# Gate matmuls of a recurrent mixer: one FP32 pass against three F32R passes over split operands

## What is computed

```python
xr = dwconv(xr, lru_conv_w[l], lru_conv_b[l], LRU_CONV_LEFT)      # 4 taps, per channel
xb = xc.reshape(b_, t_, LRU_BLOCKS, LRU_BLOCK_W)
r = jax.nn.sigmoid((jnp.einsum('btnk,nkj->btnj', xb, wa).reshape(b_, t_, ch) + ba).astype(jnp.float32))
i = jax.nn.sigmoid((jnp.einsum('btnk,nkj->btnj', xb, wx).reshape(b_, t_, ch) + bx).astype(jnp.float32))
log_a = -LRU_C * r * jax.nn.softplus(-lam.astype(jnp.float32))
a = jnp.exp(log_a)
b = jnp.sqrt(-jnp.expm1(2.0 * log_a)) * i * xc.astype(jnp.float32)
# then a scan  h = a * h + b  over context and latent tokens, in either direction
```

## Time and profile before

| | |
|---|---|
| median of the runs | 2164.99 us |
| profiled execution | 2164.49 us, span 2162.7 us |
| PE busy | 2083.7 us (96%) |
| DVE busy | 1572.5 us (73%) |
| ACT busy | 1059.2 us (49%) |
| POOL busy | 345.8 us (16%) |
| share of the last chain: PE, DVE, ACT | 79%, 11%, 4% |
| mean granted clock of TensorE | 0.995 of full speed |
| L890, 192 matmul records | 77.1 us busy |

### The profile page before, as it was taken

How to read it: one execution, slowest core, us unless ns; L and a number is a source line. 1 busy time by engine, 2 the same in 40 slices (tenths; PEclk the granted TensorE clock), 3 DMA queues, 4 the chain that set the end, 5 groups by cost and what they waited for, 6 DMA issues and landing times.

```text
span 2162.7 us, 28256 instructions
## 1 busy us (share of the span) xinstructions
PE 2083.7 (96%) x10750; PEld 1764.5 (82%) x10750; DVE 1572.5 (73%) x2780; ACT 1059.2 (49%) x1627; POOL 345.8 (16%) x234
## 2 busy tenths in 40 slices
PE   5998999999999999999998899999999999999999
PEld 1777888988888889888886788887888888888887
DVE  6688598585985967859859766668998888863433
ACT  3476666665666657666666520014444434433221
POOL 0031230221212221123023000010111111110000
PEclk9999999999999999999999999999999999999999
DMA  8421212012112120121202475363122221145552
GB/s 323 114 59 40 62 50 60 31 52 69 35 38 69 49 72 30 40 61 49 63 9 95 150 282 179 132 197 106 69 78 88 88 87 68 60 171 204 182 182 88
DMA packets 85687, 209.92 MB, mean 97 GB/s; under 512 B 24624, under 2 KB 30128, under 8 KB 85424
## 3 DMA queue, kind: packets, MB, share of 16 engines
q1 hardware_dynamic: 63360, 182.95, 24.5%
q0 software_dynamic: 5792, 20.97, 2.8%
q10 hardware_dynamic: 16400, 4.19, 0.9%
HBM read 171.39 MB, written 40.89 MB: 98 GB/s over the span
## 4 chain that ended last, share of the span: by engine, by line
PE 79%; DVE 11%; ACT 4%; issue 1%; DMA 1%; SPq 0%; ACTq 0%; DVEq 0%
PE banks L47 14%; PE banks L46 14%; PE banks L45 14%; PE banks L986 4%; PE banks L857 4%; PE banks L859 4%; PE banks L858 4%; PE banks L2145 4%; PE banks L2144 4%; PE banks L2143 4%; PE banks L890 3%; DVE probT_low L1486 2%; PE banks L948 2%; DVE prob L1478 1%; PE banks L930 1%
## 5 line engine op out<-in xcount | busy, mean ns | idle before, releaser
L45 PE MATMUL banks<-qh,xnh 128*128 128x384 f32 (+1 forms) x640 | 223.1, 349 | 0.3 <-PEq L211 0.3
L857 PE MATMUL banks<-xnh,wh 128*128 128x512 f32 (+1 forms) x536 | 211.2, 394 | 4.0 <-ACT stage L1091 3.7
L47 PE MATMUL banks<-qh,xnl 128*128 128x384 f32 (+1 forms) x640 | 207.4, 324 | 0.0
L46 PE MATMUL banks<-ql,xnh 128*128 128x384 f32 (+1 forms) x640 | 207.3, 324 | 0.0
L859 PE MATMUL banks<-xnh,wl 128*128 128x512 f32 (+1 forms) x536 | 204.3, 381 | 0.0
L858 PE MATMUL banks<-xnl,wh 128*128 128x512 f32 (+1 forms) x536 | 204.1, 381 | 0.0
L1486 DVE TENSOR_TENSOR probT_low<-banks,probT_high 128x512 fp32r<-128x512 f32 (+2 forms) x256 | 138.8, 583 | 56.2 <-ACT probT_high L1159 55.1
L1159 ACT CAST probT_high<-banks 128x512 fp32r<-128x512 f32 (+2 forms) x256 | 117.1, 510 | 59.8 <-PE banks L948 50.8
L45 PE MATMUL banks<-yh,wh 128*128 128x512 f32 x372 | 145.2, 390 | 0.9 <-DVE wl L2330 0.9
L46 PE MATMUL banks<-yl,wh 128*128 128x512 f32 x372 | 145.1, 390 | 0.0
L47 PE MATMUL banks<-yh,wl 128*128 128x512 f32 x372 | 144.7, 389 | 0.0
(11 more groups left out here) (357 smaller groups left out, 5806.3 us busy)
## 6 DMA issues: line engine op xcount, KB each, us to landing
raw<-w_ff SPq DMA_DIRECT2D x33, 512.0 KB, 3.7
raw<-w_down SPq DMA_DIRECT2D x33, 512.0 KB, 4.3
raw<-w_fm SPq DMA_DIRECT2D x32, 512.0 KB, 6.6
raw<-w_qkv SPq DMA_DIRECT2D x24, 512.0 KB, 3.9
raw<-w_mix SPq DMA_DIRECT2D x24, 512.0 KB, 5.0
h_d<-conv_d SPq DMA_DIRECT2D x22, 512.0 KB, 2.6
sw_d<-h_d SPq DMA_DIRECT2D x44, 256.0 KB, 2.9
raw<-w_modT SPq DMA_DIRECT2D x16, 512.0 KB, 5.2
```

Source lines behind the costliest of these rows:

```text
L45: pe.matmul(out, w_hi(k), x_hi(k), start=(k == 0), stop=False)
L46: pe.matmul(out, w_hi(k), x_lo(k), start=False, stop=False)
L47: last = pe.matmul(out, w_lo(k), x_hi(k), start=False, stop=(k == chunks - 1))
L857: pe.matmul(out, fh[:, s, k, :], xnh[:, k, c0:c1], start=(k == 0), stop=False)
```

## The change

The gate matmuls are made of three F32R passes like the large products. For that the gate matrices and the convolution output are split in each turn. ACT copies the high parts (`gate_weights_high`, `gate_input_high` for each segment), DVE subtracts for the low parts (`gate_weights_low`, `gate_input_low`). New semaphores `gate_hi` and `gate_lo` count them, four per turn.

The parts lie in memory that is free at that time: the split weights in slot 0 of `fl`, the low latent part in slot 0 of `fh`, the high part over `pad`, the low context part over the start of `stage`. As slot 0 now holds gate operands until the last gate group, the splits of XR move behind it: on ACT behind the gate evacuations and in front of `decays(i, 1)`, on DVE behind the first rotation. The order of MR and XR in the sequence of splits is exchanged, and SP's load of G, which waits for the XR split, moves with it. `conv_done` is counted twice per turn, once for each part of the convolution. On DVE the first `gated_input` of a middle turn stands one sum of squares earlier. POOL's mask sums wait for `gate_lo`'s fourth count instead of `conv_done`. The last output operations of the turn before stand behind the low parts of the first two segments.

```diff
+        with ExitStack() as gate_parts:
+            xcl_context = sbuf(gate_parts, "xcl_context", [P, C], F32R)
         stage = sbuf(st, "stage", [P, HALF])
...
+        with ExitStack() as gate_parts:
+            xch = sbuf(gate_parts, "xch", [P, 1288], F32R)
         pad = sbuf(st, "pad", [P, 1288])
...
+        lwh, lwl = fl[:, 0, 0:4, :], fl[:, 0, 4:8, :]
+        xcl_tokens = fh[:, 0, :, :].rearrange("p k c -> p (k c)")
...
-        ORDER = {Q0: 0, Q1: 1, Q2: 2, XR: 3, MR: 4, MN: 5, G: 6}
+        ORDER = {Q0: 0, Q1: 1, Q2: 2, MR: 3, XR: 4, MN: 5, G: 6}
...
-                pool.wait_ge(conv_done, i + 1)
+                pool.wait_ge(gate_lo, 4 * i + 4)
...
-                if d == 0 and pieces[0] == 0:
-                    pe.wait_ge(lw_in, i * 16 + 16)
-                    pe.wait_ge(conv_done, i + 1)
                 for n in pieces:
...
-                    pe.matmul(f_bank(j)[:, 0:c1 - c0], lw[:, 2 * (n // 3) + d, :], xc[:, c0:c1],
-                              start=True, stop=True).then_inc(f_full, 1)
+                    if d == 0 and n < 3:
+                        pe.wait_ge(gate_lo, 4 * i + n + 2)
+                    m = 2 * (n // 3) + d
+                    out = f_bank(j)[:, 0:c1 - c0]
+                    pe.matmul(out, lwh[:, m, :], xch_of(n % 3), start=True, stop=False)
+                    pe.matmul(out, lwh[:, m, :], xcl_of(n % 3), start=False, stop=False)
+                    pe.matmul(out, lwl[:, m, :], xch_of(n % 3), start=False, stop=True).then_inc(f_full, 1)
...
+            def gate_weights_high(i):
+                act.wait_ge(lw_in, i * 16 + 16)
+                act.copy(lwh, lw[:, :, :]).then_inc(gate_hi, 1)
+
+            def gate_input_high(i, seg):
+                c0, c1 = SEGS[seg]
+                act.wait_ge(conv_done, 2 * i + (1 if seg == 0 else 2))
+                act.copy(xch_of(seg), xc[:, c0:c1]).then_inc(gate_hi, 1)
...
                 gelu(i, 0)
+                gate_weights_high(i)
+                gate_input_high(i, 0)
                 if not last:
                     gelu(i, 1)
+                gate_input_high(i, 1)
+                gate_input_high(i, 2)
...
-                if not last:
-                    split_hi(XR, raw_count(XR, i))
                 split_hi(MR, raw_count(MR, i))
                 q_evac(i, 6)
                 gate_pieces(i, *(GATES_FIRST if first else GATES_AFTER)[6])
                 if first:
                     q_evac(i, 7)
                     gate_pieces(i, *GATES_FIRST[7])
+                if not last:
+                    split_hi(XR, raw_count(XR, i))
...
+            def gate_weights_low(i):
+                dve.wait_ge(gate_hi, 4 * i + 1)
+                dve.tensor_tensor(lwl, lw[:, :, :], lwh.bitcast(F32), ALU.subtract).then_inc(gate_lo, 1)
+
+            def gate_input_low(i, seg, first):
+                c0, c1 = SEGS[seg]
+                dve.wait_ge(conv_done, 2 * i + 2)
+                dve.wait_ge(gate_hi, 4 * i + seg + 2)
+                if seg == 0 and not first:
+                    dve.wait_ge(stage_out, i * 64)
+                dve.tensor_tensor(xcl_of(seg), xc[:, c0:c1], xch_of(seg).bitcast(F32), ALU.subtract).then_inc(gate_lo, 1)
...
                 conv(i, first)
+                gate_weights_low(i)
+                gate_input_low(i, 0, first)
+                gate_input_low(i, 1, first)
                 if not first:
                     outputs(i - 1, GROUPS_ATT - 1, False)
-                for s in range(4):
+                gate_input_low(i, 2, first)
+                early = not first and not last
+                for s in range(3):
                     head_squares(i, s)
+                if early:
+                    gated_input(i, 0)
+                head_squares(i, 3)
...
-                if not last:
-                    split_low(XR, i)
                 split_low(MR, i, last)
                 head_squares(i, 6)
...
                 rotate(1, 0, krot[0])
+                if not last:
+                    split_low(XR, i)
                 if not first:
                     head_squares(i, 7)
```

More of the change, by code:

```diff
@@ L528, in mixer_programs @@
         sinT = cst[:, P + 3 * GW + NT * HD:].rearrange("p (t f) -> p t f", f=HD)
+        lwh, lwl = fl[:, 0, 0:4, :], fl[:, 0, 4:8, :]
+        xcl_tokens = fh[:, 0, :, :].rearrange("p k c -> p (k c)")
+        xch_of = lambda seg: xch[:, (2, 5, 5)[seg] + SEGS[seg][0]:(2, 5, 5)[seg] + SEGS[seg][1]]
+        xcl_of = lambda seg: xcl_context[:, :] if seg == 0 else xcl_tokens[:, SEGS[seg][0] - C:SEGS[seg][1] - C]
         S, lower, F_ps = banks
@@ L541, in mixer_programs @@
         lw_in = sem("b_lw_in")
+        gate_hi, gate_lo = sem("b_gate_hi"), sem("b_gate_lo")
         decayed = sem("b_decayed")
@@ L1198, in turn @@
                         split_hi(u, raw_count(u, i))
+                if not first:
                     bottoms(i - 1, GROUPS_ATT - 1)
@@ L1244, in turn @@
                     gate_pieces(i, *GATES_FIRST[7])
+                if not last:
+                    split_hi(XR, raw_count(XR, i))
+                if first:
                     decays(i, 1)
@@ L1348, in conv @@
                             then(last)
-                last.then_inc(conv_done, 1)
+                    last.then_inc(conv_done, 1)
+            def gate_weights_low(i):
[8 more added lines that the diff above has]
+                dve.tensor_tensor(xcl_of(seg), xc[:, c0:c1], xch_of(seg).bitcast(F32), ALU.subtract).then_inc(gate_lo, 1)
             def head_squares(i, s):
@@ L1520, in turn @@
                     head_squares(i, 4)
-                gated_input(i, 0)
+                if not early:
+                    gated_input(i, 0)
                 complement(i, 0)
```

## The result

The changed kernel took 2176.98 us (median of four runs: 2175.06, 2175.42, 2178.53, 2178.64) against 2164.84 for the kernel before: a ratio of 1.0064, 95% interval 1.0052 to 1.0076, so 12 to 14 us slower. I had forecast 2167.0, with 2174 as the upper end. Run once more, it gave 1.0061 (1.0046 to 1.0076). The loss is clear of the noise.

The account below looks back on a forecast made before the run. By shares PE bounds the kernel, but DVE's gapless stretch sets the first exponential. First turn +2.0, middle turns -0.3, last +0.35 sum to +2.0: 2164.49 becomes 2166.5, median 2167.0 us; 8-in-10 range 2161.5 to 2174.

Parts of the forecast that it names:

- DVE's restart, 413.1 instead of 413.95: Middle turn, behind POOL's power: mean squares, power and DVE's restart all come 0.85 us earlier.
- the forecast for a middle turn: Whole middle turn: -0.05 us taken, bounds -0.3 to +0.5, in six turns -0.3.
- Rival 1: Before the first exponential: POOL's second sum holds DVE's minimum, +1.0 us in six turns, 2173.2 in all; chance 0.25.
- The XR split: Middle turn, DVE behind the first rotation: the moved subtraction adds 1.2 us, less 0.2 absorbed at a wait for ACT.
- PE's 1.4 us end as idle time: Middle turn, behind the gates: PE is 1.4 us ahead, but this becomes idle time on PE.
- rival 2: Middle turns: DVE's stretch follows ACT and PE by 1.0 to 1.4 us in six turns, about 2160; chance 0.18.
- The groups: Gate matmuls on PE: three passes take 1.04 and 1.36 us per group instead of 1.29 and 1.72.
- The middle turns' splits: Added ACT copies and DVE subtractions lie beside the first query tile, 0.8 us to spare; price 0 to +0.5, taken 0.
- rival 3: Middle turns: gate weights land 2 us late, PE waits 2 less 0.8 six times, about 2174; chance 0.07.
- First turn: +2.0, bounds 0.6 to 3.5: First turn: late gate weights delay ACT, +1.3 at its root and POOL's power; with the XR split, +2.0 us.
- Last turn: +0.35: Last turn: splits and outputs delay the third tile by 1.2 us, partly regained, leaving +0.35; bounds -0.4 and +1.2.

Follow-up runs that it names:

- e3: Changed kernel with one FP32 matmul per gate group in place of the three passes, all splits kept; 2174.14 us, ratio 1.0063.
- f1: Changed kernel with two spare DVE operations between the mean squares and the split of MR's weights; 2166.68 us, ratio 1.0021.
- h2: Kernel before with only the XR weights' cast and split moved, gates in FP32, no gate splits; 2173.09 us, ratio 1.0049.
- g4: g1 with one FP32 matmul per gate group, splits kept; 2173.08 us, ratio 1.0049.
- g1: Changed kernel with direction-1 gate groups together, XR's split beside MR's, one-input first minimum, last-turn outputs before gate splits, first-turn gate weights loaded first; 2166.88 us, ratio 1.0020.
- e2: Changed kernel with all sixteen minima of a turn written with one tensor input; 2174.98 us, ratio 1.0068.
- e1: Changed kernel with one spare DVE operation between the mean squares and the split of MR's weights; 2178.72 us, ratio 1.0075.
- e4: Changed kernel with DVE's split of XR's weights cut to 8 of 1024 columns, in the same place; 2166.45 us, ratio 1.0024.
- h3: Changed kernel with two spare DVE operations before MR's split, one-input first minimum and first-turn gate weights loaded first; 2164.64 us, ratio 1.0012.
- k1: h3 with XR's cast and split back beside MR's and the gate operands laid elsewhere in all turns but the last; 2155.50 us, ratio 0.9966.
- h1: h3 with the previous turn's outputs put ahead of the gate splits in the last turn; 2166.84 us, ratio 1.0017.
- g2: Changed kernel with direction-1 gate groups together behind the sixth query tile in middle turns, XR's split beside MR's; 2172.33 us, ratio 1.0046.

## Why the prediction was wrong

**The step that failed first: "DVE's restart, 413.1 instead of 413.95".** It followed from mean squares and power coming 0.85 earlier, with a power of unchanged length. The mean squares were earlier, by 0.66 (D). But the length was a matter of order, which I had not checked: with one cast in front of MR's split instead of two, and that cast earlier, the split was ready at 409.18, ahead of the power at 409.24. The same pair stood in the earlier trace rows as 409.80 and 409.75. I even wrote that the power ran beside the subtractions "and cost them nothing", and did not see that this held only for the one that had started. Its price was 1.03 a turn directly; e3 and f1 show it from both sides. With the order set right, in f1, the forecast for a middle turn would have held.

**Rival 1 was right in its mechanism.** POOL's sums do catch the minimum, with the rule that I had read from the earlier trace rows. The forecast put it 0.15 ahead of the second sum; it came 0.18 behind its start. The price was 0.48 and not 1.0, since L1520 was held for 0.72 and 0.24 of that was slack in front of the exponential. I had counted it as an alternative to the forecast, at 0.25; with DVE's lateness from the power it was a consequence.

**The XR split.** +1.2 - 0.2 = 1.0 forecast in B, 0.80 measured. Right in kind and nearly in size. What was missing is that the move alone, with no change on PE, already brings the hold (h2).

**"PE's 1.4 us end as idle time" was wrong.** From e3 to f1 the passes are worth 0.72 in D and, as ACT's stage and with it the sums come 0.51 earlier against DVE's minimum, 0.47 in C, 1.24 in all; from g4 to g1 it is 1.07. In the changed kernel the same earliness let the split overtake the power, which took it all back: 141.88 with FP32 gates, 142.15 with passes. So the gain of rival 2 was there. It was spent in the same turn. (f1 differs from e3 by its two spare operations too, which stand in DVE's wait for the power.)

**What was right.** The groups: 381.69 to 382.74 for 256 + 512 columns, 1.05 (forecast 1.04). The middle turns' splits: free, as h2 and e3 show. One middle turn of six is an exception, where ACT waited 3.73 for the weights and the turn took 0.46 more than its neighbours (rival 3 in small).

**First turn: +2.0, bounds 0.6 to 3.5.** Mis-sized because it is no single number: against the one trace of before, whose weights landed after 10.3, it is -1.0 with a landing after 7.5 us (e2) and +3.8 at its power with one after 10.8 (e1). At before's own landing, which the forecast had assumed, it is +3.3 at that power (e4), where I had +1.3. In the late cases a lower clock stands behind TensorE's long wait; how much of the time is the clock's was not measured. In the profiled execution it was nothing (8.5 us). The two groups of after's runs, 3.4 apart, fit the two ends, but only the profiled execution of each kernel shows a landing, so that is argued and not shown.

**Last turn: +0.35.** Measured +0.69 at its power: the outputs of the turn before, and with them the store that ACT's second square waits for, stand behind three gate splits, as said, at a higher price. The further 0.78 belongs to the clock in a stretch before the first exponential, ahead of which PE had idled 3.62; after, in two rows:

```profile
1160.00:1163.00 3.00, 2.70 (x7) 2.15 (x8) 2.97 (x6) 1.41 (x2) 2.21 (x2) 0.50 0.02 5
1163.00:1166.00 3.00, 3.00 (x9) 2.32 (x8) 2.90 (x8) 0.00 (x0) 0.00 (x0) 0.50 0.23 87
```

It isn't the change's. Over the eighteen traces the exponential comes 49.9 to 52.7 behind the power, with no relation to the edit (h3 and f1 differ there only in the first minimum, and have 52.7 and 49.9). The records of the clock sort them: among kernels with passes it is 49.9 in five with a short low stretch, as before has it, 51.0 to 51.2 in five with a longer one, as in after, and 51.4 to 52.7 in four whose clock was low at the power as well. With a short stretch the passes are therefore 0.4 ahead of before (50.31), and after lost 1.2 to the longer one. What sets its length stays open.

## What to carry to other kernels

Where two engines exclude each other, read which of a pair started first, and by how much: a lead of 0.05 us in the trace is a state that any earlier or later producer can flip, so price both orders. A buffer that a new operand borrows moves the work that used to fill it; price that move by itself (here 1.4 us a turn against a gain of 1.2) and look for another place for the operand before giving the time away. An edit that didn't change the order it was meant to change (e1) says nothing, so look at the pair in its trace before believing the time.

## What the runs showed of the hardware

- POOL's sums and a DVE operation with two tensor inputs in SBUF take turns; the later one is stretched by the other: the minimum took 0.88 for 0.16 and ended 0.02 behind the sum, the first sum 1.39 for 1.04 behind a rotation's last operation, ending 0.90 behind it. New to me was POOL's power: as the first it lets DVE's subtractions run beside it (4.17 long, and the subtraction 1.26), as the second it waits for the one that runs (5.20 and 5.23). A lead of 0.02 us is enough. It isn't so behind every operation: the second power of a turn in after (128x16, 429.78) started 0.17 behind a scan of 256 columns with two inputs (0.69 long) and took 3.20, where it takes 3.15 in the first turn.
- With a column as the scalar of a tensor_scalar, the same minimum took 0.21 in the middle of POOL's sums. But a tensor_scalar of 24 columns with one tensor input was held: two took 2.73 for 0.38 beside a mask sum (k1, first turn).
- TensorE's granted clock was at its lower level for a stretch behind every wait of 2.83 to 3.99 us for the first turn's gate operands (six traces), and behind one of three waits of 2.22 or 2.23 in the last turn (h1, not g1 and g4). It stayed at 1.00 behind waits of 1.00 and 1.18 (after and h3, the same places) and 2.00 (h2). In h1 the 1 us longer wait and the lower clock together cost 2.4 us (140.75 against 138.32), of which the wait alone was 0.9 (g1 against g2).
